# Gated linear attention scan: key-value products of two chunks back to back, head norm steps behind even chunks

## The reference

```python
k_dec = kc * jnp.exp(g_end[:, :, None] - g)

def body(state, inp):
    q_c, kd_c, v_c, ge_c = inp
    state = state * jnp.exp(ge_c)[..., None] + jnp.einsum('bshk,bshv->bhkv', kd_c, v_c)
    o = jnp.einsum('bqhk,bhkv->bqhv', q_c, state)
    return state, o

_, o = lax.scan(body, s0, (qc, k_dec, vc, g_end))
o = rms_normalize(from_chunks(o)).reshape(b_, l_, hv) * norm_w
o = o.astype(h.dtype) * jax.nn.silu(r)
return o @ w_out
```

## Time and profile before

| | us |
|---|---|
| median of 3 runs | 3349.74 (3349.42 to 3350.89) |
| profiled execution, its own time | 3348.37 |
| its span | 3346.5 |
| scan, first kv to the start of the output projection | 212.2 (2142.15 to 2354.34) |
| TensorE busy | 3123.1 (93%) |
| VectorE busy | 1380.6 (41%) |
| ScalarE busy | 739.7 (22%) |
| GpSimd busy | 483.2 (14%) |

### The profile page before, as it was taken

How to read it: one execution, slowest core, us unless ns; L and a number is a source line. 1 busy time by engine, 2 the same in 40 slices (tenths; PEclk the granted TensorE clock), 3 DMA queues, 4 the chain that set the end, 5 groups by cost and what they waited for, 6 DMA issues and landing times.

```text
span 3346.5 us, 27300 instructions
## 1 busy us (share of the span) xinstructions
PE 3123.1 (93%) x11270; PEld 1586.5 (47%) x11270; DVE 1380.6 (41%) x1780; ACT 739.7 (22%) x870; POOL 483.2 (14%) x326
## 2 busy tenths in 40 slices
PE   6988998988899999998999998999999999999997
PEld 4453445644455444444774533454444444444444
DVE  4636882358645159413762311033433343431001
ACT  3106661024300200013541122111102222220000
POOL 0004772004300000005620000000001221210000
PEclk9999998999899999999999899999999999999998
DMA  7000000020042201103321101100121111111101
GB/s 244 25 26 7 1 1 13 26 77 1 1 176 88 82 19 44 32 31 89 74 85 40 33 7 50 32 19 19 32 82 44 51 38 51 38 46 58 75 35 51
DMA packets 41067, 162.39 MB, mean 49 GB/s; under 512 B 5264, under 2 KB 5776, under 8 KB 36720
## 3 DMA queue, kind: packets, MB, share of 16 engines
q1 hardware_dynamic: 34704, 143.18, 12.3%
q0 software_dynamic: 6240, 17.47, 2.2%
HBM read 148.04 MB, written 15.20 MB: 49 GB/s over the span
## 4 chain that ended last, share of the span: by engine, by line
PE 85%; DVE 6%; ACT 3%; POOL 3%; DMA 2%; issue 1%; SPq 0%; DVEq 0%; ACTq 0%; POOLq 0%
PE ps L702 33%; PE ps L1189 15%; PE ps L1243 9%; PE ps L1123 4%; PE ps L1076 3%; PE ps L1005 2%; PE ps L922 2%; PE ps L955 2%; PE ps L850 1%; PE ps L864 1%; PE ps L835 1%; PE ps L974 1%; DMA arena<-in_wall 1%; PE ps L1100 1%; PE ps L726 1%
## 5 line engine op out<-in xcount | busy, mean ns | idle before, releaser
L702 PE MATMUL ps<-arena 128*128 128x512 f32 (+1 forms) x2784 | 1107.8, 559 | 19.7 <-ACT arena L1295 7.6
L702 PEld LDWEIGHTS ps<-arena 128*128 128x128 f32 x2784 | 530.6, 191 | 588.8 <-issue 564.1
L1243 PE MATMUL ps<-arena 128*128 128x512 f32 x616 | 264.5, 592 | 0.0
L922 PE MATMUL ps<-arena 64*128 64x512 f32 x504 | 153.6, 689 | 45.7 <-DVE x_ctx L1816 23.1
L1243 PEld LDWEIGHTS ps<-arena 128*128 128x128 f32 x616 | 117.0, 190 | 147.3 <-issue 147.3
L1892 DVE TENSOR_TENSOR x_lat<-ps,x_lat 128x1024 f32<-128x1024 f32 x16 | 19.6, 1224 | 351.8 <-PE ps L1243 279.0
L1931 DVE SCALAR_TENSOR_TENSOR x_ctx<-arena,vectors,x_ctx 128x1024 f32<-128x1024 f32 x120 | 154.2, 1285 | 4.3
L1189 PE MATMUL ps<-x_lat,arena 128*128 128x512 f32 x336 | 151.0, 592 | 0.0
L1189 PE MATMUL ps<-arena 128*128 128x512 f32 x336 | 150.9, 592 | 0.0
L1278 ACT ACTIVATE arena<-x_lat 128x1024 f32<-128x1024 f32 x40 | 42.0, 1050 | 484.3 <-DVEq L1900 484.3
L1189 PE MATMUL ps<-x_lat,x_ctx 128*128 128x512 f32 x336 | 147.6, 592 | 0.0
(11 more groups left out here) (249 smaller groups left out, 3976.0 us busy)
## 6 DMA issues: line engine op xcount, KB each, us to landing
arena<-in_wall SPq DMA_DIRECT2D x188, 512.0 KB, 3.7
arena<-expanded_bias POOLq DMA_DIRECT2D x80, 160.0 KB, 3.9
arena<-in_wdown SPq DMA_DIRECT2D x7, 1408.0 KB, 5.9
x_lat<-in_xl_in SPq DMA_DIRECT2D x8, 1024.0 KB, 9.0
residual_store<-x_lat SPq DMA_DIRECT2D x8, 1024.0 KB, 6.3
x_lat<-residual_store SPq DMA_DIRECT2D x8, 1024.0 KB, 8.6
out<-x_lat SPq DMA_DIRECT2D x8, 512.0 KB, 3.0
expanded_bias<-in_rpb POOLq DMA_DIRECT2D x1, 2560.0 KB, 17.8
```

The source lines that it names most:

```text
L702: mm = pe.matmul(ps[:, o + c:o + c + n], W[:, ring_of(g) % WSLOTS, k, :], rhs(k, c, n), start=(k == 0), stop=(k == KT - 1))
L922: mm = pe.matmul(ps[:, o:o + BANK], QK[r, 4, kt * P:(kt + 1) * P], QK[r, 0:4, c0:c1], start=True, stop=True)
L1243: mm = pe.matmul(ps[:, o + c:o + c + n], wd[:, k, :], ACTV[:, k, c:c + n], start=(k == 0), stop=(k == DOWN_K - 1))
```

## The change

On TensorE, kv(0) and kv(1) are issued ahead of the loop as before, then kv(i + 1) and kv(i + 2) together behind the r_product of each odd step and ahead of its chunk_out. A kv of an even chunk now waits until both banks have been read (`st_ready` at i); the odd one of the pair has then nothing left to wait for. head_sums moves behind step c = 9. On VectorE, head_add moves from c = 7 to 8, the four reciprocals from one each behind c = 12 to 15 to two each behind c = 12 and 14, and the two head_mix from c = 1 and 3 to c = 2 and 4. No operation is added or removed.

```diff
--- before.py
+++ after.py
@@ -1096,7 +1096,7 @@
                 h, c = divmod(i, NCH)
                 r = 64 * (c % 2)
                 if i >= 2:
-                    pe.wait_ge(st_ready, i - 1)
+                    pe.wait_ge(st_ready, i - i % 2)
                 pe.matmul(ps[:, KV_PS + (i % 2) * BANK:KV_PS + (i % 2) * BANK + GDV], GKT[r:r + 64, h, (c // 2) * P:(c // 2 + 1) * P],
                           GV[r:r + 64, c // 2, h * GDV:(h + 1) * GDV], start=True, stop=True).then_inc(kv_ready, 1)
 
@@ -1134,12 +1134,14 @@
                 mm.then_inc(gn_ps, 1)
 
             kv(0)
+            kv(1)
             for i in range(steps):
-                if i + 1 < steps:
+                r_product(i)
+                if i % 2 and i + 2 < steps:
                     kv(i + 1)
-                r_product(i)
+                    kv(i + 2)
                 chunk_out(i)
-                if i % NCH == 8 and i >= NCH:
+                if i % NCH == 9 and i >= NCH:
                     head_sums(i // NCH - 1)
 
             pe.wait_ge(r_free, 8)
@@ -2004,14 +2006,15 @@
                 else:
                     dve.scalar_tensor_tensor(STATE[:, i % 2, :], STATE[:, (i - 1) % 2, :], DEC[:, h, c:c + 1], kv,
                                              ALU.mult, ALU.add).then_inc(st_ready, 1)
-                if h and c == 7:
+                if h and c == 8:
                     head_add(h - 1)
                 if h and c == 10:
                     head_mean(h - 1)
-                if h and c >= 12:
+                if h and c in (12, 14):
                     head_reciprocal(h - 1, c - 12)
-                if h > 1 and c in (1, 3):
-                    head_mix(h - 2, c // 2)
+                    head_reciprocal(h - 1, c - 11)
+                if h > 1 and c in (2, 4):
+                    head_mix(h - 2, c // 2 - 1)
             for j in range(2):
                 head_mix(2, j)
             head_add(3)
```

## The result

The changed kernel takes 3355.45 us in the median of 22 runs (3347.67 to 3362.45), the kernel before 3348.67 in 22 runs (3345.62 to 3356.88): ratio 1.0018, 95% interval 1.0012 to 1.0025. It is slower by 0.2%, where 3342.9 was forecast. (A ratio here comes from all runs with its interval; it need not be the quotient of the two medians.) The profiled execution took 3353.93, against 3348.37.

A forecast was written before the change was run, and what follows sets the result against it. TensorE was taken to set the pace, with VectorE's state chain hidden. Pairs -17.9, reciprocal stall +8.6 and clock +2.5 sum to -6.8 us: 3342.9 against the median 3349.74, range 3337.0 to 3348.0.

The forecast's parts named there:

- The clock term: TensorE's scan gaps: 4.5 falls of the granted clock replace 3, +2.5 us, bounds -5.0 and +5.0.
- The pairs: TensorE's scan: 31 kv pairs at 0.79 against 0.77 per single kv, saving 17.9 us over eight stretches.
- rival C: The 31 pairs: row halves don't overlap in mid-stream, pair cost up to 1.41, slower at 3357.7 us; 5%.
- A's own range: Main forecast, 77%: change of -12 to -3 us, from clock terms and 0.1 either way on 24 pairs.
- The silu waits: TensorE's line 1123 in the scan: seven waits grow by 0.64, from 11.7 to 16 us in all.
- The reciprocals: VectorE behind state 12: two in a row delay state 13, stalling kv 14 by 2.86 in three heads, +8.6 us.
- T + 6.66: Forecast time when state 13 is done, in us after the start of the evacuation (2232.50).
- Rival B: VectorE's reciprocals stay hidden; only the 17.9 saving and longer old gaps remain: 3332 us; 8%.
- D: Second stall at c = 14, TensorE waiting for state 15, 1 us in three heads: 3346 us; 10%.
- Head_add, head_mean and the mixes: Moved head norm steps: no stall; mixes hidden by 0.8 before the next pair.
- "Slower": Whole kernel: outcome slower than the kernel before by over 0.2%, chance 0.04.
- the new wait: Sign in the scan: TensorE (line 1100) waits for VectorE's state of line 2005, three times, 2.8 us each.

The follow-up runs named there:

- filled scan: Scan with useless TensorE instructions in idle gaps; for 207.24, the kernel before with them at its three 2.49 us silu waits: 3345.82 us, ratio 0.9990.
- all_filled: Changed kernel plus useless TensorE instructions at the seven silu waits and in the three waits of kv 14 for state 13: 3335.77 us, ratio 0.9962.
- recip_odd: Changed kernel with two reciprocals each behind states 13 and 15 instead of 12 and 14: 3340.34 us, ratio 0.9969 to the kernel before.

## Why the prediction was wrong

**The clock term failed.** It was put at +2.5 us: 4.5 falls replace 3, and of the gaps of 1.07, which grow to 1.7, "I take nothing"; its bound was +5.0. Scan against filled scan gives the measured size: 212.19 - 207.24 = 4.95 us in the kernel before, 216.65 - 199.25 (all_filled) = 17.40 after, so the clock adds 12.4 us and not 2.5. That is past the bound as well: with +5.0 the sum would still have been -4.3, a faster kernel. Three things were missed. The four gaps of 1.69 do bring the clock down, three of four here and eleven of sixteen over all traces. The gaps of 2.8 and 3.1 do so more often than three in four, 20 of 21. And two of the falls in the changed kernel are twice as long. I had three falls of three behind gaps of 2.49 and none of four behind 1.07, with nothing between, and set the 1.7 with the 1.07 for no reason but their order; the bound belonged at a fall behind all ten gaps of the changed scan, seven more than three and 11.6 us, not at three more.

**The pairs** were right in kind, and their saving was put 1.5 us too high: 24.55 - 22.50 = 2.05 per stretch of eight steps, 16.4 for eight, against 17.9. The pair itself takes 0.63 as the start of the scan showed (rival C falls); what is dearer is the output behind it, 0.49 to the next r product and not 0.44. The 0.03 that was estimated for the second increment from the Trainium skill ("TensorE: Matmul & The Clock Gate", The cost: per-tile semaphore tail) is not seen: a single kv takes 0.63 as well. Rival C and A's own range counted 24 pairs where the sum has about four in each of eight stretches. By the sum itself C would have decided from a pair cost of 1.00 and not 1.10, and at its bound of 1.41 the stage would have lost some 2 us instead of saving 3.1.

**The silu waits** were right: they grew from 1.07 and 2.49 to 1.69 and 3.11, since the kv that filled a part of each now runs ahead of it.

**The reciprocals** were right to 0.04: the root's wait ends 3.00 behind the evacuation, the pair of reciprocals and the state are done at T + 6.66, and the stall is 2.82 us, three times. In the timeline of head 1 (evacuation, two reciprocals, state 13, pair):

```profile
2228.91 0.66 PE L1111 MATMUL ps<-arena 128*128 128x64 f32 x4
...
2229.60 0.60 ACT L1478 ACTIVATE arena<-ps 128x512 f32<-128x512 f32 x1 [14.08 <-PE ps L1111]
...
2232.60 3.36 DVE L1987 RECIPROCAL arena<-arena 128x256 f32<-128x256 f32 x2 [3.11 <-ACT arena L1473]
2235.88 0.38 DVE L2007 SCALAR_TENSOR_TENSOR arena<-arena,chunk_decay,ps 128x256 f32<-128x256 f32 x1
...
2236.32 1.01 PE L1100 MATMUL ps<-arena 64*128 64x256 f32 x4 [2.82 <-DVE arena L2007]
```

Rival B falls. The kv pairs wait for VectorE only three times, never for state 15, so D falls too. Head_add, head_mean and the mixes cost nothing on the path.

**The sum by measured terms**: -16.4 + 8.5 + 12.4 = +4.5 us, which is what the scan shows (216.65 - 212.19). The forecast of -6.8 had the pairs, the silu waits and the stall right, and its sign was decided by the term with the fewest rows behind it. "Slower", at 0.04, had as its only mechanism pairs that don't overlap. That the four short gaps would cross into the range where the clock falls was not among the rivals. Of the signs that were named, the new wait and the longer silu waits came; the clock fell behind nine gaps of the scan and not four or five, and the scan takes 216.65 us and not 205.

## What to carry to other kernels

A change that moves work out of a wait of TensorE, or makes TensorE wait anew, lengthens its idle gaps. Here the clock fell behind gaps of 1.69 us in 11 of 16 cases, and each fall cost 1.7 us, as much again as the gap. So it paid to put short independent products into a wait and not ahead of it. Where none was left, useless ones helped: ten fillers turned a kernel of 3355 us into one of 3336. When small steps of one engine are gathered in groups, place the group where the next result of that engine is due latest: with the reciprocals behind odd chunks (recip_odd) the stall of 8.5 us was gone.

## What the runs showed of the hardware that was not expected

The clock fell behind gaps much shorter than the prediction had reckoned with. The table counts the gaps of the scan and the output projection in all thirteen traces:

| gap, us | falls | gaps |
|---|---|---|
| 0.7 to 1.1 | 0 | 34 |
| 1.2 to 1.35 | 1 | 26 |
| 1.58 (ahead of the first kv) | 0 | 13 |
| 1.69 | 11 | 16 |
| 2.48 | 8 | 12 |
| 2.82 | 8 | 9 |
| 3.02 (ahead of the output projection) | 7 | 12 |
| 3.11 | 12 | 12 |

Of the twelve at 3.11 three are of double length and one is three times as long. That the gap of 3.02 has fewer falls than the one of 2.82, and the one of 1.58 none, shows that length is not all; which gaps are spared was not settled. Executions of one program differ by 10 us and more, and the clock goes with it: of the 22 runs of the changed kernel the fastest (3347.67) had a granted clock of 0.960 and the slowest (3362.45) 0.954.
